# Memory attention worked head by head between the query tiles, with its output projection begun per head

## What is computed

```python
def memory_cross_attention(h, mem_n, w_q, w_kv, w_o):
    q = (h @ w_q).reshape(b, s, MEM_HEADS, MEM_HEAD_DIM)          # 4 heads of 128
    kv = (mem_n @ w_kv).reshape(b, m, 2, MEM_HEADS, MEM_HEAD_DIM)  # m = 256
    k, v = kv[:, :, 0], kv[:, :, 1]
    sc = jnp.einsum('bqhd,bmhd->bhqm', q, k, preferred_element_type=jnp.float32) * (MEM_HEAD_DIM ** -0.5)
    p = jax.nn.softmax(sc, axis=-1)
    o = jnp.einsum('bhqm,bmhd->bqhd', p.astype(v.dtype), v).reshape(b, s, MEM_WIDTH)
    return o @ w_o

for l in range(2):
    x = x + hybrid_mixer(...)
    x = x + memory_cross_attention(rms_norm(x, norm_mem_q[l]), rms_norm(mem, norm_mem_kv[l]), ...)
    x = x + conv_ffn(rms_norm(x, norm_ffn[l]), w_up[l], ...)
```

## Time and profile before

| what | us |
|---|---|
| median of 3 runs | 2336.4 (2331.95 to 2340.49) |
| profiled execution, its own time | 2341.49 |
| span of its trace | 2339.7 |
| busy: PE, DVE, ACT, POOL | 2253.1, 1539.6, 1187.0, 603.2 |
| granted TensorE clock, mean | 0.989 of full speed |

### The profile page before, as it was taken

How to read it: one execution, slowest core, us unless ns; L and a number is a source line. 1 busy time by engine, 2 the same in 40 slices (tenths; PEclk the granted TensorE clock), 3 DMA queues, 4 the chain that set the end, 5 groups by cost and what they waited for, 6 DMA issues and landing times.

```text
span 2339.7 us, 48313 instructions
## 1 busy us (share of the span) xinstructions
PE 2253.1 (96%) x19152; PEld 2135.6 (91%) x19152; DVE 1539.6 (66%) x2490; ACT 1187.0 (51%) x1849; POOL 603.2 (26%) x741
## 2 busy tenths in 40 slices
PE   8999999899999999899999999998999999999998
PEld 7889999799999789899998899997889998798998
DVE  5656555656554776665556565658768976767994
ACT  5555544445544643455345555444556554556653
POOL 1114221003211030121111142117135535134540
PEclk9999999999999999999999999999999999999999
DMA  5224545324545321255452345563344555343554
GB/s 208 93 91 165 177 159 193 103 87 163 180 153 191 124 67 63 73 174 171 158 181 94 108 156 186 170 208 136 119 179 149 193 167 177 108 145 127 184 173 130
DMA packets 53007, 344.03 MB, mean 147 GB/s; under 512 B 5920, under 2 KB 7136, under 8 KB 20448
## 3 DMA queue, kind: packets, MB, share of 16 engines
q1 hardware_dynamic: 52128, 336.26, 43.4%
q0 software_dynamic: 704, 5.31, 0.6%
HBM read 340.43 MB, written 1.05 MB: 146 GB/s over the span
## 4 chain that ended last, share of the span: by engine, by line
PE 78%; DVE 9%; ACT 6%; issue 4%; DMA 2%; POOL 2%; DVEq 0%; SPq 0%; ACTq 0%; POOLq 0%
PE ps L773 76%; ACT ring_hi L1527 3%; DVE ring_lo L2091 3%; ACT arena L1527 1%; PE ps L979 1%; POOL arena L2999 1%; POOL arena_r L3000 1%; DMA ring<-in 0%; ACT y_r L1527 0%; DVE x L2142 0%; DVE newt L2113 0%; DMA ring<-out 0%; DVE newt L2107 0%; PE ps L1413 0%; DVE arena L2771 0%
## 5 line engine op out<-in xcount | busy, mean ns | idle before, releaser
L773 PE MATMUL ps<-arena_r,ring_hi 128*128 128x272 f32 (+1 forms) x6688 | 1578.0, 286 | 9.9 <-DVE arena_r L2603 5.5
L773 PEld LDWEIGHTS ps<-arena_r,ring_hi 128*128 128x128 f32 x6688 | 1156.4, 189 | 18.3 <-issue 11.3
L773 PE MATMUL ps<-y_r,ring_hi 128*128 128x272 f32 (+1 forms) x3424 | 1008.3, 294 | 20.4 <-POOL arena_r L3000 10.3
L2091 DVE TENSOR_TENSOR ring_lo<-ring,ring_hi 128x2048 fp32r<-128x2048 f32 (+3 forms) x373 | 739.6, 1984 | 362.9 <-ACT ring_hi L1527 362.3
L773 PE MATMUL ps<-y_r,ring_lo 128*128 128x272 f32 (+1 forms) x3424 | 976.3, 285 | 0.0
L773 PEld LDWEIGHTS ps<-y_r,ring_hi 128*128 128x128 f32 x3424 | 649.1, 190 | 45.0 <-issue 13.6
L1527 ACT ACTIVATE ring_hi<-ring 128x2048 fp32r<-128x2048 f32 (+3 forms) x373 | 611.6, 1643 | 91.3 <-DMA ring<-dn 47.9
L773 PEld LDWEIGHTS ps<-y_r,ring_lo 128*128 128x128 f32 x3424 | 650.6, 190 | 0.0
L773 PE MATMUL ps<-arena_r,ring_lo 128*128 128x256 f32 (+1 forms) x1632 | 462.6, 283 | 0.0
L773 PEld LDWEIGHTS ps<-arena_r,ring_lo 128*128 128x128 f32 x1632 | 307.6, 188 | 0.0
L1527 ACT ACTIVATE arena<-arena 128x272 f32<-128x272 f32 (+7 forms) x197 | 91.0, 464 | 392.7 <-DVE arena L2675 262.3
(11 more groups left out here) (242 smaller groups left out, 1698.7 us busy)
## 6 DMA issues: line engine op xcount, KB each, us to landing
ring<-gu SPq DMA_DIRECT2D x88, 1024.0 KB, 5.1
ring<-dn SPq DMA_DIRECT2D x64, 704.0 KB, 4.0
ring<-up SPq DMA_DIRECT2D x44, 1024.0 KB, 5.1
ring<-fox_in SPq DMA_DIRECT2D x31, 1024.0 KB, 5.2
ring<-sdn SPq DMA_DIRECT2D x32, 704.0 KB, 4.1
ring<-gdn_in SPq DMA_DIRECT2D x16, 1024.0 KB, 5.2
ring<-in SPq DMA_DIRECT2D x16, 1024.0 KB, 5.2
ring<-gla_in SPq DMA_DIRECT2D x12, 1024.0 KB, 5.1
```

The costliest lines, as they stand in the source:

```text
L773: return nc.tensor.matmul(dst, w, mv, start=start, stop=stop)
L2091: V.tensor_tensor(ring_lo[:, slot, cols], ring[:, slot, cols], ring_hi[:, slot, cols].bitcast(F32), ALU.subtract).then_inc(lo_ready, 2 if ...
```

## The change

It rewrites the three blocks' middle for each engine:

- TensorE: `memory` takes the place of `memory_q`, `attention` and memo's `project_out`. The q tiles use two banks (0 and 1); banks 2 and 3 hold scores, one head in each, 4 and 5 transposes, 6 and 7 outputs. All transposes of v stand ahead of the last chunk of tile 0. Scores of head t-1 stand in the middle of tile t, the transposes of head 0 behind tile 2, its values in the middle of tile 3. The output projection does its chunk k for the first four output tiles as soon as head k is ready, then finishes these four one after the other; tiles 4 to 7 follow whole.
- The heads are worked whole (two query halves at once). q is evacuated with the negative scale, so that the lowest score is the bias of the exponent: one reduction for a head, no second instruction. VectorE makes only the inverse; **GpSimd scales p**. ScalarE makes the high part of a head's output straight from PSUM, VectorE the low part.
- The split of up's first half is moved from memo's residuals into the attention: on ScalarE between the copy of head 1's transposes and the exponents of head 3, on VectorE ahead of the last head's low part. The split of the second half is moved behind the last square (ScalarE) and behind the last residual and sum (VectorE).

The diff, cut to its core (the removed functions are those printed above):

```diff
+            def memory(nb, tpb, kc):
+                v_tile, first_tile = n.tile - 12, n.tile
+                def values_to_tokens():
+                    pe.wait_ge(evacuated, BANKS + v_tile + 4)
+                    for c in range(4):
+                        for q in range(2):
+                            at = (2 * (c % 2) + q) * P
+                            last = nc.tensor.transpose(ps[:, 4 + c // 2, at:at + P], m_v[:, c, q * P:(q + 1) * P], ident)
+                        if c % 2:
+                            last.then_inc(vt_ready, 2)
+                def scores(h):
+                    pe.wait_ge(evacuated, BANKS + first_tile + h + 1)
+                    if h >= 2:
+                        pe.wait_ge(exp_ready, n.unit + 2 * h - 2)
+                    for r in range(2):
+                        mm(ps[:, 2 + h % 2, r * SEQ:(r + 1) * SEQ], m_q[:, h, r * P:(r + 1) * P], m_k[:, h, :]).then_inc(s_ready, 1)
+                def turn(h):
+                    pe.wait_ge(p_ready, n.unit + 2 * h + 2)
+                    if h >= 2:
+                        pe.wait_ge(ptok_ready, n.unit + 2 * h - 2)
+                    else:
+                        pe.wait_ge(vtok_ready, n.vtok + 2 * h + 2)
+                    for q in range(2):
+                        for r in range(2):
+                            at = (2 * q + r) * P
+                            last = nc.tensor.transpose(ps[:, 4 + h % 2, at:at + P], memory_p(h, r)[:, q * P:(q + 1) * P], ident)
+                    last.then_inc(pt_ready, 2)
+                def values(h):
+                    pe.wait_ge(ptok_ready, n.unit + 2 * h + 2)
+                    pe.wait_ge(vtok_ready, n.vtok + 4)
+                    if h >= 2:
+                        pe.wait_ge(out_split, n.split + h - 1)
+                    for q in range(2):
+                        last = mm(ps[:, 6 + h % 2, 0:SEQ], m_vtok[:, q, h * P:(h + 1) * P], flat(memory_pt(h)[:, 2 * q:2 * q + 2, :]), q == 0, q == 1)
+                    last.then_inc(pv_ready, 2)
+                def project(k, t):
+                    half, at = divmod((4 * t + k) * P, SLOT)
+                    slot = (2 * n.block + half) % SLOTS
+                    hi, lo = ring_hi[:, slot, at:at + P], ring_lo[:, slot, at:at + P]
+                    dst = acc(n.tile + t, SEQ)
+                    mm(dst, hi, m_hi_r[:, k, :], k == 0, False)
+                    mm(dst, hi, a_o_r[:, k, :], False, False)
+                    return mm(dst, lo, m_hi_r[:, k, :], False, k == 3)
+                def ahead(k, tiles):
+                    pe.wait_ge(out_split, n.split + k + 1)
+                    for t in tiles:
+                        project(k, t)
+                def ready(k):
+                    if k == KC - 1:
+                        values_to_tokens()
+                    y_chunk(k)
+                def middle(t):
+                    if t == 3:
+                        values(0)
+                    if t:
+                        scores(t - 1)
 
                 def after(t):
...
+                    if t == 2:
+                        turn(0)
+                blocks(nb, tpb, kc, y_parts2, SEQ, ready, after, 2, middle)
+                free = [t for t in range(4) if (n.tile + t) % BANKS < 2]
+                scored = [t for t in range(4) if t not in free]
+                turn(1)
+                pe.wait_ge(evacuated, BANKS + n.tile)
+                pe.wait_ge(lo_ready, quarters(2 * n.block, 1))
+                ahead(0, free)
+                scores(3)
+                values(1)
+                turn(2)
+                ahead(1, free)
+                values(2)
+                turn(3)
+                pe.wait_ge(exp_ready, n.unit + 8)
+                ahead(0, scored)
+                values(3)
+                ahead(1, scored)
+                ahead(2, range(4))
+                pe.wait_ge(out_split, n.split + 4)
+                for t in range(4):
+                    project(3, t).then_inc(acc_ready, 1)
+                pe.wait_ge(lo_ready, quarters(2 * n.block + 1, 1))
+                for t in range(4, 8):
+                    pe.wait_ge(evacuated, n.tile + t + 1)
+                    for k in range(4):
+                        last = project(k, t)
+                    last.then_inc(acc_ready, 1)
+                n.tile += 8
+                n.block += 1
                 n.vtok += 4
...
+                n.unit += 8
+                n.split += 4
+                new_norm(SEQ)
...
-                    memory_q(name, nb, tpb, kc)
...
+                    memory(nb, tpb, kc)
...
+                if late is not None:
+                    split(late, 1)
                 ln_exp()
...
+            def memory(name, before):
+                l = int(name[-1])
+                def take_tokens(b):
+                    act.wait_ge(vt_ready, n.vtok + 2 * b + 2)
+                    dst = m_vtok[:, :, b * 2 * P:(b + 1) * 2 * P].rearrange("p q (c d) -> p c q d", d=P)
+                    fn(dst, ps[:, 4 + b, :].rearrange("p (c q d) -> p c q d", c=2, q=2), ACT.Copy).then_inc(vtok_ready, 2)
+                def exponents(h):
+                    if h >= 2:
+                        act.wait_ge(pt_ready, n.unit + 2 * h - 2)
+                    for r in range(2):
+                        at = memory_slot(h, r)
+                        act.wait_ge(max_ready, n.unit + 2 * h + r + 1)
+                        fn(memory_p(h, r), ps[:, 2 + h % 2, r * SEQ:(r + 1) * SEQ], ACT.Exp, scale=-1.0, bias=neg_max[:, at:at + 1],
+                           accum_out=row_sum[:, at:at + 1]).then_inc(exp_ready, 1)
+                def take_turned(h):
+                    act.wait_ge(pt_ready, n.unit + 2 * h + 2)
+                    if h >= 2:
+                        act.wait_ge(pv_ready, n.unit + 2 * h - 2)
+                    fn(flat(memory_pt(h)), ps[:, 4 + h % 2, :], ACT.Copy).then_inc(ptok_ready, 2)
+                def high(h):
+                    act.wait_ge(pv_ready, n.unit + 2 * h + 2)
+                    fn(m_hi_r[:, h, :], ps[:, 6 + h % 2, 0:SEQ], ACT.Copy).then_inc(memory_high, 1)
+                before(0)
+                take_tokens(0)
+                take_tokens(1)
+                exponents(0)
+                before(2)
+                exponents(1)
+                take_turned(0)
+                high(0)
+                exponents(2)
+                take_turned(1)
+                split(n.block + 2, 0)
+                exponents(3)
+                high(1)
+                take_turned(2)
+                high(2)
+                take_turned(3)
+                high(3)
+                n.tile += 4
+                n.vtok += 4
+                n.unit += 8
...
-                    norm_x(xs if second else x, GAINS[name], SEQ if second else T, n.tile, before, name == "sdn1")
+                    late = n.block + 1 if name.startswith("memo") else None
+                    norm_x(xs if second else x, GAINS[name], SEQ if second else T, n.tile, before if late is None else (lambda c: None), name == "sdn1", late)
...
+            def memory(name, after):
+                l = int(name[-1])
+                def evacuate(c):
+                    v.wait_ge(acc_ready, n.tile + c + 1)
+                    V.scalar_tensor_tensor(out=m_q[:, c, :], in0=acc(n.tile + c, SEQ, P, 2), scalar=-(float(P) ** -0.5), in1=rstd[:, 0:SEQ],
+                                           op0=ALU.mult, op1=ALU.mult).then_inc(evacuated, 1)
+                def smallest(h):
+                    at = memory_slot(h, 0)
+                    v.wait_ge(s_ready, n.unit + 2 * h + 2)
+                    V.tensor_reduce(neg_max[:, at:at + 2], ps[:, 2 + h % 2, :].rearrange("p (r k) -> p r k", r=2), AX.X, ALU.min).then_inc(max_ready, 2)
+                def inverse(h):
+                    if h >= 2:
+                        v.wait_ge(p_ready, n.unit + 2 * h - 2)
+                    for r in range(2):
+                        at = memory_slot(h, r)
+                        v.wait_ge(exp_ready, n.unit + 2 * h + r + 1)
+                        V.reciprocal(row_inv[:, at:at + 1], row_sum[:, at:at + 1]).then_inc(inv_ready, 1)
+                def low(h):
+                    v.wait_ge(memory_high, 4 * l + h + 1)
+                    V.tensor_tensor(a_o_r[:, h, :], ps[:, 6 + h % 2, 0:SEQ], m_hi_r[:, h, :].bitcast(F32), ALU.subtract).then_inc(out_split, 1)
+                new_rstd(SEQ)
+                evacuate(0)
+                after(0)
+                smallest(0)
+                evacuate(1)
+                inverse(0)
+                smallest(1)
+                evacuate(2)
+                inverse(1)
+                after(2)
+                smallest(2)
+                low(0)
+                evacuate(3)
+                inverse(2)
+                smallest(3)
+                low(1)
+                inverse(3)
+                low(2)
+                split(n.block + 2, 0)
+                low(3)
+                n.tile += 4
+                n.vtok += 4
+                n.unit += 8
...
```

(17 more changed lines are left out.)

154 lines of the change are left out of this document (9 added, 145 removed).

## The result

| | before | changed |
|---|---|---|
| median of 20 runs each, us | 2337.97 (2331.78 to 2344.39) | 2342.54 (2336.45 to 2347.25) |
| ratio of times | | 1.0021, 95% interval 1.0013 to 1.0028 |
| span of the profiled execution, us | 2339.7 | 2341.4 |

The changed kernel is 0.21% slower (3.0 to 6.5 us). The forecast was 2336.6 and its range ended at 2342.5. By the bound of 0.3% that is no change, but it lies 5.9 us above the forecast, and just outside its range. Of these 5.9 us, 1.6 are the starting point: the forecast was built on a median of 3 runs, 2336.4, and that of 20 is 2337.97. The other 4.4 are the change itself: +0.2 forecast, +4.6 measured.

What follows compares the result with a forecast made beforehand. TensorE, busy 2253.1 of 2339.7 us, was taken to bound the kernel. Profiled 2341.49 - 1.9 - 0.5 (schedule) + 2.6 (clock) = 2341.7; that execution lay 5.1 above the median, so 2336.6 us, range 2329 to 2342.5.

Steps and rivals of the forecast that it cites:

- schedule -2.4 us: Norm before the up projection: GpSimd's chain ends earlier in both layers, 2.4 us gained in sum.
- clock +2.6: Up's tile 0, second layer: longer waits newly bring TensorE's clock down, 2.6 us lost, between 0 and 2.9.
- in the first layer the fall is paid already: Start of up, first layer: the kernel before already runs at half clock there, so only the second layer's fall is new.
- -1.9 and -0.5 forecast: GpSimd's norm chain before up ends earlier: 1.9 us gained in the first layer, 0.5 in the second.
- The wait of 1.6 us for the first evacuation: Middle of q tile 1: TensorE's first scores newly wait 1.6 us for the first q tile's evacuation.
- The 1.5 us for head 1's low part: Output projection, chunk 1: TensorE waits 1.5 us at 2121.2, behind head 3's exponents and lowest scores and up's first split.
- The hold of p of head 1: Attention: GpSimd's second scaling is held by VectorE's second weight split, done at 2116.4, asked for at 2117.8, so hidden.
- The hold of the seventh by the late split: GpSimd's norm chain: the seventh chunk's first operation is held beside VectorE's moved split until 2141.7, 1.75 us lost.
- The three waits of 1.1, 1.1 and 2.9: Up's tile 0, both layers: TensorE waits about 1.1, 1.1 and 2.9 us, with granted clock 0.5 behind them.
- The second and third: Rivals: clock holds in second layer, 2334.0, chance 0.17; split misses GpSimd's chain, clock holds in both layers, 2327.9, chance 0.15.
- The fourth, a fall inside the attention: Rival: clock falls at the 1.6 or 1.5 us waits, 1.3 to 2.9 us each, 2340.8 up to 2345; chance 0.13.
- The fifth: Rival: heads late by held p or longer reduction, output projection 2 us later in each layer, 2340; chance 0.10.

Runs made afterwards that it cites:

- e4: Changed kernel with idle products (3, 3, 10) ahead of chunks 4, 5 and 6 of up's first tile; 2335.66 us, ratio 0.9992 to the kernel before.
- e5: Kernel before with idle products (3, 3, 4) ahead of chunks 4, 5 and 6 of up's first tile; 2335.71 us, ratio 0.9995.
- e9: Kernel before, own attention, second half of up's first weights split behind GpSimd's seven chunks, idle products (3, 3, 2); 2332.17 us, ratio 0.9984.
- e3: Changed kernel with v's eight transposes ahead of chunk 6 of q tile 0 instead of chunk 7; 2339.57 us, ratio 1.0000 to the kernel before.
- e1: Changed kernel with both weight splits of up's first block back in the output projection's residuals; 2343.99 us, ratio 1.0023 to the kernel before.
- e6: Changed kernel with head 1's high and low parts ahead of head 3's exponents and lowest score; 2344.48 us, ratio 1.0024 to the kernel before.
- e12: Changed kernel with up's two splits back in the residual, v turned one chunk earlier, idle products (10, 4, 3); 2338.1 us, ratio 1.0003.
- e7: Changed kernel with second split behind GpSimd's last low part, v turned one chunk earlier, idle products (3, 3, 2); 2331.27 us, ratio 0.9976.
- e11: e7 with first scores at the end of q tile 1 and VectorE's output weight split behind head 1's lowest score; 2329.93 us, ratio 0.9969.
- e2: Changed kernel with VectorE's late second split started only after GpSimd's seven low parts; 2336.73 us, ratio 0.9989 to the kernel before.
- e8: Changed kernel with head 0's scores at q tile 1's end, VectorE's evacuation 1, lowest score and inverse before its weight split; 2341.07 us, ratio 1.0017.

## Why the prediction failed where it did

**The sum in two terms.** Forecast: schedule -2.4 us, clock +2.6, together +0.2. Measured: schedule 0 to -1 (-0.1 ± 1.0 at equal clock), clock +4.4 to +5.4. With idle products in both kernels they differ by -0.03% (e4 to e5; at equal clock e4 is 1.9 us slower, ± 1.6), so here too no gain of 2.4 shows. Both terms were mis-sized, the schedule by 1.3 to 2.3 us and the clock by 1.8 to 2.8, in the same direction.

**The clock: the step that failed is "in the first layer the fall is paid already".** It was read off one execution of the kernel before, in which 1.91 us at 1727.26 and the three waits at up's start were each followed by half speed. That execution's mean clock is 0.989, and only 16 of the 111 runs were that low or lower. e5 shows the average: idle products at up's start raise the kernel before's mean clock by 0.0003 over both layers, a fifth of one fall (1.3 us by the medians, not 2.6). In the changed kernel the same remedy raises it by 0.003, two falls, and brings 7 us (e4; interval some 3 us either way). So on average nearly both falls are new, one in each layer; that the profiled executions show only one new one is the chance of the one before. Twice 2.6 for once 2.6, and the clock term would have been right: the price of a fall was about right (e4's 7 us are 3.4 for each by medians, 2.5 by means), the number of new ones wasn't.

**The wait ahead of the q norm is no property of the kernel.** In the nine kernels that have nothing new ahead of it it took 0.97, 1.08, 1.18, 1.20, 1.21, 1.91, 1.92, 1.99 and 2.01 us. Granted clock in the 6 us behind it, kernel before, changed, e5 and e9 (waits 1.91, 1.99, 1.20, 2.01):

```profile
1727.30:1733.30 6.00, 6.00 (x37) 5.78 (x37) 3.78 (x7) 4.09 (x5) 0.00 (x0) 0.72 0.05 18
...
1722.60:1728.60 6.00, 5.33 (x28) 4.94 (x28) 1.65 (x5) 3.25 (x4) 0.00 (x0) 0.72 0.04 14
...
1724.80:1730.80 6.00, 5.95 (x49) 5.86 (x50) 3.98 (x7) 5.43 (x7) 0.00 (x0) 1.00 0.34 97
...
1722.70:1728.70 6.00, 6.00 (x49) 5.90 (x50) 3.99 (x7) 5.43 (x7) 0.00 (x0) 1.00 0.19 37
```

With the waits of 1.21 us and less the clock stayed up behind them in each of the five; with 1.9 to 2.0 it fell in three of four. All nine have the same code up to this place, so a fall of one execution can't be booked as paid in all. That the point at which the clock changes varies between runs of one kernel is what the Trainium skill says (TensorE: Matmul & The Clock Gate, What's actually happening); it says so of the rise at a kernel's start, these rows show it of a fall.

**The schedule: -1.9 and -0.5 forecast.** Second layer, counted from the norm's sum as it would be without the transposes of v: 2100.66 (2101.45 less the 0.79 between 2100.22 and the next product). The chain of GpSimd starts 28.6 us later (laid out: 28.1; before: 27.0) and takes 12.2 (11.9; before: 13.6); 40.7 us in all, for 40.6 in the kernel before. The hold that left the chain made it 1.4 us shorter, and the attention gave that back by a later start; the 0.5 us forecast are gone in two small errors. First layer, from the restart ahead of chunk 6: 43.2 us (1722.64 to 1765.81) for 42.9 before, laid out 40.9. Of the missing 2.2, 1.6 lie ahead of the first scores, which start 6.7 us behind the restart (1729.35) and not 5.1. The transposes of v stood right behind the wait and met the slow clock (1.55 us to the next product, not 0.8), and so did chunk 7 and the norm's sum behind them. Tile 1, slow in the kernel before, was fast again by then, and what it saved went into the wait for the first evacuation, 1.38 us and not 0.5. The rest is the later start of the second layer once more. e3 takes the transposes away and is 0.2% faster than the changed kernel.

**Right.** The wait of 1.6 us for the first evacuation (1.44; its own terms, 2103.4 + 0.44 + 1.4 = 2105.2 and not 2105.1, give 1.5). The 1.5 us for head 1's low part (1.40), though not by the split I named among its causes: e1 leaves it at 1.40, the exponents and the lowest score of head 3 make it, and e6 only hands it on. The hold of p of head 1 (3.02 us for a pair that takes 0.94), which TensorE doesn't wait for. The reduction of 512 columns at 0.70 (0.70 on the chain). The pace of a GpSimd chunk, 1.45 (1.47, from 2129.21 to 2138.04 for six). The hold of the seventh by the late split (2.52; said: over 2), with no hold before it. The three waits of 1.1, 1.1 and 2.9, if a third shorter in the first two (0.75, 0.82, 2.68), and that they bring the clock down in both layers.

**The rivals.** The second and third needed the clock to hold; it didn't. The fourth, a fall inside the attention, does not stand in the changed kernel's trace (two falls at up's start and one at the q norm of the first layer), but did happen in e6. Its price range, 2340.8 to 2345, holds the result all the same, by luck: the falls were elsewhere. (Four falls at the larger price of 2.9 would make 2348.2, not 2345.) The fifth asked for an output projection 2 us late in each layer: GpSimd's chain behind it began 0.4 us later than laid out in the second and 2.1 in the first (31.0 for 28.9), so it holds for the first alone, and there by the clock, not by a held p or a long reduction. What is left open is how often each of these falls happens, since one execution of a kernel has a trace.

**What the parts are worth**, with the clock held up, at equal clock: the attention of the change with splits in the residual +3.9 us (e12 to e5); with the late split behind GpSimd -1.2 (e7 to e9); the late split behind GpSimd alone -1.3 (e9 to e5); VectorE's order in e11 another -2.6 (e11 to e7). Each has an interval of 1.2 to 1.5 us either way, so the first and the last are clear of zero and the two between barely. By the ratios the same four are +1.9, -1.9, -2.6 and -1.6, each with 3 us either way, none of them clear of zero. What is sure is the sum from the kernel before over e5, e9 and e7 to e11: 0.31%, which its interval sets apart from zero.

## What to carry to other kernels

A change that starts a bound engine's stage earlier, while what feeds it ends as before, turns one kind of loss into waits, and on TensorE waits can cost a second time, through the clock (two falls in the changed kernel); put work that is due anyway (e3) or idle products (e4) into them before judging the schedule. Don't take a clock fall of one profiled execution for a property of the kernel: compare the mean granted clock of many runs, and the time at equal clock. A large VectorE operation on two SBUF tiles belongs behind GpSimd's chain (e2), not behind VectorE's own last piece of work.

## What the runs showed of the hardware

- The granted clock, averaged over an execution, explains most of the spread between runs of one kernel (0.73 of its variance in 111 runs): 0.987 to 0.993 and 2343 to 2334 us.
- In the changed kernel's second layer three waits of 0.75, 0.82 and 2.68 us with only three products between them brought the clock down; e2's 0.75, 0.81 and 0.65 did as well; 0.50, 0.91 and 1.08 in the kernel before did not the earlier trace rows.
- A pair of GpSimd operations (128x256, scaling) that takes 0.94 us takes 2.97 beside a VectorE weight split of 2.34 (e8), and 3.02 beside one of 2.29 (changed kernel).
